# Two attentions in one queue: another order of their events, the selection's last steps among them, squares by ScalarE

## The chip, the cores and the metric

One core of one Trainium2 chip. The kernel is a single launch; its time is the device time in microseconds (us), the median of several runs. Before the change three runs took 2541.43, 2534.55 and 2539.69 us, median 2539.69 us.

## The reference

Two transformer blocks, one after the other, on 1024 tokens of width 1024, all in float32. The change lies in the first block, in two of its three mixers:

```
h = x @ w_in                                   # all mixers' inputs
# differential attention: 4 heads, 2 maps of 64 columns each, values 128 wide
p = softmax(q k^T * scale - slope * |i - j|, chunk-causal mask)      # per map
attn = p[map 0] - lam * p[map 1]
o = rms_norm(attn @ v over 128 columns, subln_g) * (1 - lam_init)
# sparse attention: 4 heads of 64 columns
score = sum over 8 heads of w_i * relu(q_i k_i^T)
sel = the 256 best keys of each query by score # blocks 0 and 1 take all their keys
out = softmax(q k^T * scale - slope * |i - j|, over sel) @ v
x = layer_norm(a * x + concat(gmlp, o, out) @ w_out)
```

Behind this stand a gated feed-forward layer and the whole second block; neither is touched.

## The kernel before

Each engine has its own program, written out by hand: `pe_program` (TensorE), `act_program` (ScalarE), `dve_program` (VectorE), `pool_program` (GpSimd) and `sp_program` (SyncE, which issues all DMAs). An engine works its program strictly in order; waits on semaphores tie them together. Queries are worked in 8 blocks of 128; block i sees 128 (i + 1) keys.

The stage before the attentions projects x (48 steps, `pe_project`) and beside that finds each query's 256th best score bit by bit (`dve_topk`). When the threshold of a query is known, `dve_choose` turns the scores of a block into a bias, block by block for i = 2 to 7: five VectorE instructions (lines 1194 to 1208) that mark ties, count them by a running sum, drop those that are too many, and write 0 or a large negative number plus the distance over the scores. Blocks 2 to 5 are done at the end of `dve_topk`, with `running` as their buffer; blocks 6 and 7 inside the attention loop, one instruction at each place from the second on, with `tcum` as buffer.

The attentions are 48 events: 32 differential ones ("b", head, block) and 16 sparse ones ("c", pair of heads, block). Every event has two maps: in "b" the two maps of a head, in "c" the two heads of a pair. The list `events` gives each event its place t. Each engine goes through places 0 to 54, and at place t it does different steps of several events:

- TensorE (`pe_attend`): the logits of event t, both maps (line 1296); the product with the values of event t - 4 (line 1386); the turning over (transposes) of event t - 2 (line 1360).
- VectorE (`dve_attend`): the logits' bias, scale and row maximum for each map of event t (line 1321), which empties TensorE's banks; the scaling of a sparse event t - 4 (line 1410), between the two maps; the reciprocal of the sums of event t - 1 and, for "b", the joining of its two maps (lines 1338 to 1346); for a head whose last block was 5 places ago the mean squares (lines 1419 to 1423, with `tcum`), and 6 places ago the scaling of its whole output (line 1440).
- ScalarE (`act_attend`): the exponentials of event t (line 1330), the scaling of a "b" event t - 4 (line 1400), the copies of the turned maps of event t - 2 (line 1372), and a square root 5 places behind a head's last block (line 1428).
- SyncE (`sp_attend`): first the loads of heads 1 and 4, then, 5 places behind, the stores of finished sparse outputs and further loads of heads, 6 places behind the stores of a finished head; behind the last head's stores the loads of the mixed blocks (`sp_mix_in`).

A "b" event turns one map (the joined one), a "c" event two. The banks are two rings: logits in 4 banks, turned maps and products in 4. An event of more than 512 keys takes all 4 banks of the first ring. The values of a map lie in one of eight buffers `vals`, which together are `res`.

The operands of a head (queries and keys in two parts each, and values) are five loads of 512 KB into one of three stacks (`sp_load_head`, lines 1277 and 1279): differential heads n = 0 to 3 into stacks 0 and 1 in turn, the two sparse pairs, n = 4 and 5, into stack 2. TensorE waits for all five before an event's logits (`pe_logits`, line 1287). Head 0 is loaded in the stage before. The loads of heads 1 and 4 stand behind the projection's last stores, first head 1, then head 4.

Behind the attentions `pe_mix` turns the mixed blocks that come back from DRAM: block 0 before the last event's product, the others behind it.

Of the kernel before, what the change touches and what calls it, by code (L numbers as in the profile page):

```python
# [166 lines left out]
def rest(*streams):  # L167
    for s in streams:
        for _ in s:
            pass  # L170


def build(nc, T, out):
    with ExitStack() as top:
# [91 lines left out]
        junk = sb("junk", 1024, BF, 512)  # L266
        junk_a = sb("junk_a", 1024, BF, 512)
        sg, powers = sb("sg", 128), sb("powers", 32)
        running = res[:, 7168:8192]


        area(low)
# [879 lines left out]
        def dve_topk():  # L1152


            dve.wait_ge(*BITS_BANK["r"].prior("bits"))
            for n, i in BY_DVE + BY_ACT:
                dve.i.memset(limit[:, n:n + 1], cols[i][1] - (256.0 if n < 3 else 512.0)).then_inc(*dv.up())
            dve.i.tensor_copy(bits, powers[:, 0:31].bitcast(U32)).then_inc(*dv.up())
            dve_count(BY_DVE + BY_ACT, None, ALU.is_ge)
            dve.wait_ge(*dv.now())  # L1160
            dve.i.tensor_scalar(ci, cnt, 256.0, -1.0, ALU.is_lt, ALU.mult).then_inc(*dv.up())
            dve.wait_ge(*dv.now())
            dve.i.tensor_tensor(cu, cu, bits[:, 30:31].broadcast_to([128, 6]), ALU.bitwise_xor).then_inc(*dv.up(("threshold", 30)))
            for b in BITS:
                dve_count(BY_DVE, cand[:, 0:6], ALU.is_lt)
                dve.wait_ge(*av.after(("signs", b)))
                dve.wait_ge(*dv.now())
                dve.i.tensor_tensor(rj, cnt, limit, ALU.is_gt).then_inc(*dv.up())
                dve.wait_ge(*dv.now())
                dve.i.scalar_tensor_tensor(out=cu, in0=rj, scalar=b, in1=cu, op0=ALU.logical_shift_left, op1=ALU.bitwise_xor  # L1170
                                           ).then_inc(*dv.frees(uses, "bits"))
                if b:
                    dve.wait_ge(*dv.now())
                    dve.i.tensor_tensor(cu, cu, bits[:, b - 1:b].broadcast_to([128, 6]), ALU.bitwise_xor
                                        ).then_inc(*dv.up(("threshold", b - 1)))
                yield
            dve_next_up()
            dve_count(BY_DVE + BY_ACT, cand[:, 0:6], ALU.is_gt)
            dve.wait_ge(*dv.now())
            dve.i.tensor_scalar(need, cnt, -1.0, 256.0, ALU.mult, ALU.add).then_inc(*dv.up())  # L1180
            yield
            for i in range(2, 6):
                rest(dve_choose(i, running))
                yield
            while True:
                yield

        def dve_choose(i, sums):

            n = COLUMN[i]  # L1190
            o, ln = cols[i]
            sc, thr, jk = score[:, o:o + ln], cand[:, n:n + 1], junk[:, 0:ln]
            dve.wait_ge(*dv.now())
            dve.i.tensor_scalar(jk, sc, thr, None, ALU.is_equal).then_inc(*dv.up())
            yield
            dve.wait_ge(*dv.now())
            dve.i.tensor_tensor_scan(sums[:, 0:ln], jk, jk, 0.0, ALU.add, ALU.bypass).then_inc(*dv.up())
            yield
            dve.wait_ge(*dv.now())
            dve.i.scalar_tensor_tensor(out=jk, in0=sums[:, 0:ln], scalar=need[:, n:n + 1], in1=jk, op0=ALU.is_gt,  # L1200
                                       op1=ALU.mult).then_inc(*dv.up())
            yield
            dve.wait_ge(*dv.now())
            dve.i.scalar_tensor_tensor(out=sc, in0=sc, scalar=thr, in1=jk, op0=ALU.is_lt, op1=ALU.add).then_inc(*dv.up())
            yield
            dve.wait_ge(*nd_in.after("nd"))
            dve.wait_ge(*dv.now())
            dve.i.scalar_tensor_tensor(out=sc, in0=sc, scalar=-BIG, in1=nd[:, 896 - 128 * i:1024], op0=ALU.mult, op1=ALU.min
                                       ).then_inc(*dv.up(("chosen", i)))
            yield  # L1210
# [3 lines left out]

        b_events = [("b", h, i) for h in range(4) for i in range(8)]
        c_events = [("c", p, i) for p in range(2) for i in range(8)]
        events = b_events[0:8]

        events += [e for pair in zip(b_events[8:16], c_events[0:8]) for e in pair] + b_events[16:20]
        events += [e for pair in zip(b_events[20:24], b_events[24:28]) for e in pair]  # L1220
        events += [e for pair in zip(b_events[28:32], c_events[8:12]) for e in pair] + c_events[12:16]
        N_EVENT = len(events)
        place_of = {e: t for t, e in enumerate(events)}
        turned_uses = [(t, m) for t, e in enumerate(events) for m in range(1 if e[0] == "b" else 2)]
# [167 lines left out]
        def act_outputs(t):  # L1392
            kind, g, i = events[t]
            tile = (t, "out")
            act.wait_ge(*dv.after((t, "rc")))
            act.wait_ge(*mm.after((t, 0, "out")))
            for k in range(4):
                act.wait_ge(*stage_out[k].after(("v", CV0 + 4 + k)))
            act.wait_ge(*osb_out[g % 2].after(("b", g - 2)))
            act.i.activation(osb[g % 2][:, 128 * i:128 * i + 128], uses.held[tile][:, 0:128], ACT.Copy,  # L1400
                             scale=small((t, "rc"), 2)[:, 0:1]).then_inc(*av.frees(uses, tile))

        def dve_outputs(t):
            kind, g, i = events[t]
# [7 lines left out]
                                rc.unsqueeze(2).broadcast_to([128, 2, 64]), ALU.mult).then_inc(*dv.frees(uses, tile))  # L1412


        def dve_subln(h):
            ss, ob = small(("subln", h), 24), osb[h % 2]
            dve.wait_ge(*av.after((place_of["b", h, 7], "out")))
            dve.wait_ge(*dv.now())
            dve.i.tensor_tensor(tcum[:, :], ob[:, :], ob[:, :], ALU.mult).then_inc(*dv.up())
            dve.wait_ge(*dv.now())  # L1420
            dve.i.tensor_reduce(ss[:, 0:8], tcum.rearrange("p (n c) -> p n c", n=8), AX.X, ALU.add).then_inc(*dv.up())
            dve.wait_ge(*dv.now())
            dve.i.tensor_scalar(ss[:, 0:8], ss[:, 0:8], 1.0 / 128, LN_EPS, ALU.mult, ALU.add).then_inc(*dv.up(("subln_var", h)))

        def act_subln(h):
# [61 lines left out]

        def dve_attend():

            last_choices = chain(dve_choose(6, tcum), dve_choose(7, tcum), repeat(None))  # L1490
            for t in range(N_PLACES):
                if t < N_EVENT:
                    dve_logits(t, 0)
                u = lagging(t, 4, "c")
                if u is not None:
                    dve_outputs(u)
                if t < N_EVENT:
                    dve_logits(t, 1)
                u = lagging(t, 1)
                if u is not None:  # L1500
                    dve_sums(u)
                    next(last_choices)
                h = last_block(t, 5)
                if h is not None:
                    dve_subln(h)
                h = last_block(t, 6)
                if h is not None:
                    dve_subln_end(h)
# [1428 lines left out]
```

## Time and profile before

| | |
|---|---|
| runs, median (lowest to highest) | 2539.69 us (2534.55 to 2541.43) |
| profiled execution, its own time | 2536.39 us |
| its span | 2534.4 us |
| TensorE, VectorE, ScalarE, GpSimd busy | 2403.1, 1491.6, 944.3, 688.5 us |
| TensorE's mean granted clock | 0.976 of full speed |
| attention stage, first logits to last product | 345 to 567 us |

The clock column of a window (PEclk) is the TensorE clock that was granted, as a share of the full 2.4 GHz; 0.50 is 1.2 GHz. Busy time of TensorE at half clock is twice that of the same work at full clock. A row of a timeline gives the start from the span's beginning, the length, the engine, line and operation, and in brackets how long the engine had been idle and what ended that.

### The profile page before, as it was taken

The page shows a single profiled execution, that of the slowest core. Times are in us where ns is not written, and L with a number is a line of the kernel's source. Part 1 is how long each engine was busy: PE and PEld are TensorE (multiplying, and loading weights), DVE is VectorE, ACT ScalarE, POOL GpSimd, SP SyncE. Part 2 cuts the span into 40 slices and gives each one's busy share as a digit, 9 for nine tenths or more (in the row PEclk, how much of TensorE's full clock was granted, in tenths as well). Part 3 has the DMA queues.
Part 4 walks back from the last instruction along what each step waited for, and adds up shares of the span by engine and source line. Part 5 has one row for each costly group of instructions (what it writes and reads, how often), then busy time and mean ns, then how long its engine had stood idle before and what let it go on. Part 6 is the DMA issues. An engine that isn't in the chain of part 4 may idle for free.

```text
span 2534.4 us, 31471 instructions
## 1 busy us (share of the span) xinstructions
PE 2403.1 (95%) x12119; PEld 1944.2 (77%) x12119; DVE 1491.6 (59%) x2500; ACT 944.3 (37%) x1762; POOL 688.5 (27%) x389
## 2 busy tenths in 40 slices
PE   8999968889999999999999989888989999999998
PEld 6678857777887777778887866666868888888887
DVE  3588998762766777753239037775476555544225
ACT  3467836661223232222113225553433233332112
POOL 3022210001135445542223211012224444442220
PEclk9999978999999999999999999998989999999999
DMA  5026441224215455454222210001332222233233
GB/s 173 9 64 195 161 156 56 96 66 147 103 56 154 154 158 158 146 202 166 91 100 75 75 42 18 26 18 67 100 94 73 84 75 92 84 133 117 100 108 116
DMA packets 216860, 260.00 MB, mean 103 GB/s; under 512 B 16364, under 2 KB 145916, under 8 KB 216712
## 3 DMA queue, kind: packets, MB, share of 16 engines
q1 hardware_dynamic: 216712, 258.00, 31.0%
q8 instruction: 96, 1.57, 0.3%
q14 instruction: 52, 0.43, 0.1%
HBM read 198.14 MB, written 59.82 MB: 102 GB/s over the span
## 4 chain that ended last, share of the span: by engine, by line
PE 55%; DVE 8%; DMA 2%; ACT 1%; issue 1%; POOL 1%; POOLq 0%; SPq 0%; DVEq 0%; ACTq 0%
PE bank L545 8%; PE bank L546 8%; PE bank L547 8%; PE bank L1878 7%; PE bank L1879 7%; PE bank L1880 7%; DVE rest L2498 3%; PE bank L521 2%; PE bank L523 2%; PE bank L522 2%; DMA early<-in_w_cond 1%; DVE took L2503 1%; DVE macc L1675 1%; POOL wl L502 1%; PE bank L2426 1%
## 5 line engine op out<-in xcount | busy, mean ns | idle before, releaser
L502 POOL TENSOR_TENSOR wl<-raw,wh 128x1024 fp32r<-128x1024 f32 x117 | 296.5, 2550 | 1338.8 <-ACT wh L485 1318.8
L545 PE MATMUL bank<-wh,yh 128*128 128x512 f32 x768 | 301.6, 393 | 3.7 <-POOL wl L502 1.7
L546 PE MATMUL bank<-wl,yh 128*128 128x512 f32 x768 | 299.5, 390 | 0.0
L547 PE MATMUL bank<-wh,yl 128*128 128x512 f32 x768 | 299.5, 390 | 0.0
L485 ACT ACTIVATE wh<-raw 128x1024 fp32r<-128x1024 f32 x117 | 123.2, 1057 | 311.0 <-PE bank L547 292.1
L497 POOL TENSOR_TENSOR wl<-res,wh 128x512 fp32r<-128x512 f32 x144 | 198.4, 1400 | 147.0 <-ACT wh L482 126.7
L1878 PE MATMUL bank<-yh,wh 128*128 128x512 f32 x576 | 225.2, 391 | 0.0
L1880 PE MATMUL bank<-yh,wl 128*128 128x512 f32 x576 | 224.1, 389 | 0.0
L1879 PE MATMUL bank<-yl,wh 128*128 128x512 f32 x576 | 224.1, 389 | 0.0
L497 POOL TENSOR_TENSOR wl<-raw,wh 128x512 fp32r<-128x512 f32 x108 | 156.3, 1461 | 232.1 <-ACT wh L482 232.1
L2077 DVE TENSOR_TENSOR res<-bank,res 128x512 f32<-128x512 f32 x96 | 65.6, 690 | 192.2 <-PE bank L547 192.2
L2011 DVE TENSOR_TENSOR res<-bank,res 128x512 f32<-128x512 f32 x144 | 99.6, 692 | 132.2 <-PE bank L1880 124.5
L545 PEld LDWEIGHTS bank<-wh,yh 128*128 128x128 f32 x768 | 144.6, 188 | 35.8 <-issue 5.4
L547 PEld LDWEIGHTS bank<-wh,yl 128*128 128x128 f32 x768 | 144.5, 188 | 30.2
L546 PEld LDWEIGHTS bank<-wl,yh 128*128 128x128 f32 x768 | 144.7, 188 | 29.2
L521 PE MATMUL bank<-yh,wh 128*128 128x512 f32 x384 | 153.6, 400 | 9.8 <-DVE yl L582 8.3
L482 ACT ACTIVATE wh<-res 128x512 fp32r<-128x512 f32 x144 | 83.4, 623 | 192.5 <-DVE res L469 141.4
L523 PE MATMUL bank<-yh,wl 128*128 128x512 f32 x384 | 150.8, 393 | 0.0
L522 PE MATMUL bank<-yl,wh 128*128 128x512 f32 x384 | 150.7, 392 | 0.0
L1878 PEld LDWEIGHTS bank<-yh,wh 128*128 128x128 f32 x576 | 108.1, 188 | 30.0 <-issue 4.3
L1880 PEld LDWEIGHTS bank<-yh,wl 128*128 128x128 f32 x576 | 108.1, 188 | 22.7
L1879 PEld LDWEIGHTS bank<-yl,wh 128*128 128x128 f32 x576 | 108.1, 188 | 22.1
(343 smaller groups left out, 5395.9 us busy)
## 6 DMA issues: line engine op xcount, KB each, us to landing
early<-in_w_cond SPq DMA_DIRECT2D x96, 256.0 KB, 3.0
raw<-in_w_gu SPq DMA_DIRECT2D x44, 512.0 KB, 4.2
raw<-in_w_down SPq DMA_DIRECT2D x44, 512.0 KB, 3.6
raw<-in_w_in SPq DMA_DIRECT2D x40, 512.0 KB, 4.1
qk_d<-res SPq DMA_DIRECT2D x36, 512.0 KB, 4.2
raw<-in_w_gate SPq DMA_DIRECT2D x22, 512.0 KB, 4.1
raw<-in_w_up SPq DMA_DIRECT2D x22, 512.0 KB, 4.3
res<-in_x SPq DMA_DIRECT2D x16, 512.0 KB, 10.0
```

Source lines behind the costliest of these rows:

```text
L485: act.i.activation(wh[n % NU][:, :], raw_of(u)[:, :], ACT.Copy).then_inc(*av.up(("wh", u)))
L497: pool.i.tensor_tensor(wl[n % NU][:, half], src, wh[n % NU][:, half].bitcast(F32), ALU.subtract).then_inc(*po.up(("wl", u)))
L502: pool.i.tensor_tensor(wl[n % NU][:, :], raw_of(u)[:, :], wh[n % NU][:, :].bitcast(F32), ALU.subtract).then_inc(*po.up(("wl", u)))
L521: pe.i.matmul(bank[:, :], a, a_h[:, s], start=k == 0, stop=False)
L522: pe.i.matmul(bank[:, :], a, a_l[:, s], start=False, stop=False)
L523: last = pe.i.matmul(bank[:, :], b, a_h[:, s], start=False, stop=k == 7)
L545: pe.i.matmul(bank[:, 0:wide], xa, h[:, c:c + wide], start=k == 0, stop=False)
L546: pe.i.matmul(bank[:, 0:wide], xa, l[:, c:c + wide], start=False, stop=False)
L547: last = pe.i.matmul(bank[:, 0:wide], xb_, h[:, c:c + wide], start=False, stop=k == nk - 1)
L1878: pe.i.matmul(bank[:, :], h[:, c:c + 128], high[:, k, :], start=k == 0, stop=False)
L1879: pe.i.matmul(bank[:, :], h[:, c:c + 128], low[:, k, :], start=False, stop=False)
L1880: last = pe.i.matmul(bank[:, :], l[:, c:c + 128], high[:, k, :], start=False, stop=k == 3)
```

## The change

The order of the events: two differential ones and one sparse one from the first place on, through places 0 to 23; then head 2's first six blocks alone; then again two to one, and the last three sparse events alone. The choices of blocks 2 to 5 leave `dve_topk` and join those of blocks 6 and 7 in the attention loop: 30 instructions, handed out at places 5 to 22 by `chosen_by`, all with `tcum` as buffer. VectorE takes the logits of both maps before it scales a sparse event's output. The squares of a differential head's output and their sums are no longer two VectorE instructions on the whole head, but one ScalarE activation with accumulation for each event, beside the one that scales it.

```diff
--- before.py
+++ after.py
@@ -266,7 +266,6 @@
         junk = sb("junk", 1024, BF, 512)
         junk_a = sb("junk_a", 1024, BF, 512)
         sg, powers = sb("sg", 128), sb("powers", 32)
-        running = res[:, 7168:8192]
 
 
         area(low)
@@ -1179,9 +1178,6 @@
             dve.wait_ge(*dv.now())
             dve.i.tensor_scalar(need, cnt, -1.0, 256.0, ALU.mult, ALU.add).then_inc(*dv.up())
             yield
-            for i in range(2, 6):
-                rest(dve_choose(i, running))
-                yield
             while True:
                 yield
 
@@ -1214,11 +1210,10 @@
 
         b_events = [("b", h, i) for h in range(4) for i in range(8)]
         c_events = [("c", p, i) for p in range(2) for i in range(8)]
-        events = b_events[0:8]
-
-        events += [e for pair in zip(b_events[8:16], c_events[0:8]) for e in pair] + b_events[16:20]
-        events += [e for pair in zip(b_events[20:24], b_events[24:28]) for e in pair]
-        events += [e for pair in zip(b_events[28:32], c_events[8:12]) for e in pair] + c_events[12:16]
+
+
+        events = [e for n in range(8) for e in (b_events[2 * n], b_events[2 * n + 1], c_events[n])] + b_events[16:22]
+        events += [e for n in range(5) for e in (b_events[22 + 2 * n], b_events[23 + 2 * n], c_events[8 + n])] + c_events[13:16]
         N_EVENT = len(events)
         place_of = {e: t for t, e in enumerate(events)}
         turned_uses = [(t, m) for t, e in enumerate(events) for m in range(1 if e[0] == "b" else 2)]
@@ -1397,8 +1392,11 @@
             for k in range(4):
                 act.wait_ge(*stage_out[k].after(("v", CV0 + 4 + k)))
             act.wait_ge(*osb_out[g % 2].after(("b", g - 2)))
-            act.i.activation(osb[g % 2][:, 128 * i:128 * i + 128], uses.held[tile][:, 0:128], ACT.Copy,
-                             scale=small((t, "rc"), 2)[:, 0:1]).then_inc(*av.frees(uses, tile))
+            bank, rc = uses.held[tile], small((t, "rc"), 2)[:, 0:1]
+            act.i.activation(osb[g % 2][:, 128 * i:128 * i + 128], bank[:, 0:128], ACT.Copy, scale=rc).then_inc(*av.up())
+            act.wait_ge(*av.now())
+            act.i.activation(junk_a[:, 0:128], bank[:, 0:128], ACT.Square, scale=rc,
+                             accum_out=small(("subln", g), 24)[:, i:i + 1]).then_inc(*av.frees(uses, tile))
 
         def dve_outputs(t):
             kind, g, i = events[t]
@@ -1412,14 +1410,10 @@
                                 rc.unsqueeze(2).broadcast_to([128, 2, 64]), ALU.mult).then_inc(*dv.frees(uses, tile))
 
 
+
         def dve_subln(h):
-            ss, ob = small(("subln", h), 24), osb[h % 2]
+            ss = small(("subln", h), 24)
             dve.wait_ge(*av.after((place_of["b", h, 7], "out")))
-            dve.wait_ge(*dv.now())
-            dve.i.tensor_tensor(tcum[:, :], ob[:, :], ob[:, :], ALU.mult).then_inc(*dv.up())
-            dve.wait_ge(*dv.now())
-            dve.i.tensor_reduce(ss[:, 0:8], tcum.rearrange("p (n c) -> p n c", n=8), AX.X, ALU.add).then_inc(*dv.up())
-            dve.wait_ge(*dv.now())
             dve.i.tensor_scalar(ss[:, 0:8], ss[:, 0:8], 1.0 / 128, LN_EPS, ALU.mult, ALU.add).then_inc(*dv.up(("subln_var", h)))
 
         def act_subln(h):
@@ -1487,19 +1481,23 @@
 
         def dve_attend():
 
-            last_choices = chain(dve_choose(6, tcum), dve_choose(7, tcum), repeat(None))
+            choices = chain.from_iterable(dve_choose(i, tcum) for i in range(2, 8))
+
+            def chosen_by(t):
+                return min(30, max(0, 5 * (t - 4) // 3))
+
             for t in range(N_PLACES):
                 if t < N_EVENT:
                     dve_logits(t, 0)
+                    dve_logits(t, 1)
                 u = lagging(t, 4, "c")
                 if u is not None:
                     dve_outputs(u)
-                if t < N_EVENT:
-                    dve_logits(t, 1)
                 u = lagging(t, 1)
                 if u is not None:
                     dve_sums(u)
-                    next(last_choices)
+                    for _ in range(chosen_by(t) - chosen_by(t - 1)):
+                        next(choices)
                 h = last_block(t, 5)
                 if h is not None:
                     dve_subln(h)
```

## Rows read from the trace of the kernel before

**Rows 1.** The page, part 1: busy time of each engine over the span

```profile
PE 2403.1 (95%) x12119; PEld 1944.2 (77%) x12119; DVE 1491.6 (59%) x2500; ACT 944.3 (37%) x1762; POOL 688.5 (27%) x389
```

**Rows 2.** Windows: length; busy PE, PEld, DVE, ACT, POOL; PEclk; DMA share; GB/s

```profile
345.40:362.20 16.80, 0.53 (x10) 0.33 (x6) 16.38 (x16) 2.33 (x4) 4.88 (x2) 0.61 0.69 249
362.20:402.00 39.80, 32.30 (x191) 25.62 (x192) 37.53 (x103) 23.33 (x67) 0.00 (x0) 0.69 0.16 57
402.00:453.00 51.00, 45.39 (x339) 37.22 (x338) 38.56 (x124) 36.70 (x86) 0.00 (x0) 0.90 0.22 71
453.00:503.00 50.00, 43.64 (x332) 36.07 (x332) 36.44 (x128) 34.28 (x90) 0.00 (x0) 0.93 0.35 119
503.00:547.00 44.00, 38.13 (x290) 31.57 (x290) 33.84 (x109) 33.24 (x78) 0.00 (x0) 0.92 0.06 19
547.00:567.00 20.00, 17.90 (x146) 17.76 (x147) 4.97 (x17) 7.99 (x16) 0.00 (x0) 0.91 0.42 142
```

**Rows 3.** Timeline of TensorE where the stage begins: start, length, idle before

```profile
362.48 0.69 PE L1296 MATMUL bank<-kh,qh 64*128 64x384 f32 x2 [16.55 <-DVE st L1321]
```

**Rows 4.** Timeline of the DMA issues of SyncE in the same stretch

```profile
354.60 3.44 SPq L1277 DMA_DIRECT2D qh<-qk_d  x1
...
359.52 0.43 SPq L1279 DMA_DIRECT2D v<-v_d  x1
```

**Rows 5.** Windows of 2 us, where the DMA engines fall quiet

```profile
368.00:370.00 2.00, 0.92 (x6) 0.23 (x6) 1.96 (x7) 0.90 (x3) 0.00 (x0) 0.50 0.18 47
```

**Rows 6.** Timeline of VectorE through the choices of blocks 2 to 5

```profile
340.01 0.42 DVE L1194 TENSOR_SCALAR junk<-score,cand 128x384 bf16<-128x384 f32 x1
...
345.22 2.86 DVE L1200 SCALAR_TENSOR_TENSOR junk<-res,cand,junk 128x512 bf16<-128x512 f32 x1
348.12 2.71 DVE L1204 SCALAR_TENSOR_TENSOR score<-score,cand,junk 128x512 f32<-128x512 f32 x1
...
360.96 0.96 DVE L1208 SCALAR_TENSOR_TENSOR score<-score,nd 128x768 f32<-128x768 f32 x1
```

**Rows 7.** Groups of VectorE's instructions from 340 to 567 us, shapes apart

```profile
L1419 DVE TENSOR_TENSOR tcum<-osb 128x1024 f32<-128x1024 f32 x4 | 4.9, 1225 | 0.4
L1421 DVE TENSOR_REDUCE st<-tcum 128x8 f32<-128x1024 f32 x4 | 4.9, 1220 | 0.1
...
L1410 DVE TENSOR_TENSOR osc<-bank,st 128x128 f32<-128x128 f32 x16 | 4.7, 291 | 27.5 <-PE bank L1386 27.5
```

**Rows 8.** Windows cut where TensorE's granted clock changes

```profile
379.00:389.00 10.00, 6.81 (x56) 5.43 (x52) 9.24 (x22) 6.11 (x13) 0.00 (x0) 0.96 0.01 2
389.00:396.00 7.00, 6.68 (x36) 5.97 (x36) 6.79 (x14) 4.25 (x12) 0.00 (x0) 0.57 0.00 0
...
420.00:470.00 50.00, 46.78 (x395) 40.92 (x396) 29.75 (x102) 32.58 (x79) 0.00 (x0) 0.99 0.12 40
```

**Rows 9.** Timeline of TensorE in the second half and at the end

```profile
475.52 0.47 PE L1296 MATMUL bank<-kh,qh 64*128 64x128 f32 x2 [4.05 <-DVE st L1321]
...
515.14 0.44 PE L1296 MATMUL bank<-kh,qh 64*128 64x384 f32 x2 [2.35 <-DVE st L1321]
...
551.22 2.79 PE L1386 MATMUL bank<-v,pt 128*128 128x64 f32 x24
...
560.53 1.94 PE L564 MATMUL bank<-con,ms 128*128 128x128 f32 x8 [1.70 <-DMA ms<-mix_d]
```

**Rows 10.** Timeline of VectorE: the last head's scaling

```profile
550.59 2.19 DVE L1440 SCALAR_TENSOR_TENSOR osb<-osb,st,sg 128x128 f32<-128x128 f32 x8
```

**Rows 11.** Groups of ScalarE's instructions from 345 to 567 us, shapes apart

```profile
L1330 ACT ACTIVATION_READ_ACCUMULATOR res<-res,st 128x1 f32 x96 | 18.2, 190 | 0.0
...
L1400 ACT ACTIVATE osb<-bank,st 128x128 f32<-128x128 f32 x32 | 11.3, 352 | 0.1
...
L1330 ACT ACT_TABLE_LOAD x4 | 5.1, 1283 | 0.1
```

**Rows 12.** Groups of ScalarE's instructions over the whole span

```profile
L631 ACT ACTIVATE sq<-res 128x1024 bf16<-128x1024 f32 x31 | 32.8, 1058 | 52.6 <-DVE res L2077 28.0 <-DVE res L2656 12.0 <-DVE res L627 11.9
```

## The prediction

> **What bounds the kernel now.** The page's first part [rows 1] shows TensorE busy for 2403.1 of 2534.4 us; the attention stage, the only place that the change touches, holds its longest pause. So I cut that stage into windows [rows 2], then read the timelines of TensorE [rows 3, 9], SyncE's issues [rows 4], the DMA engines [rows 5] and VectorE [rows 6, 7, 10] in it.
>
> Three stretches are to be seen. (a) 345.9 to 362.5: TensorE stands still for 16.55 us [rows 3], because VectorE makes the choices of blocks 2 to 5, from 340.01 to 361.92 [rows 6], before it touches the first logits. (b) Places 0 to 23 (heads 0 and 1 of the differential attention, head pair 0 of the sparse one), 362.2 to 453.0 us: VectorE is busy 37.53 + 38.56 = 76.1 of 90.8 us. TensorE is busy 32.30 + 45.39 us, but at mean clocks of 0.69 and 0.90; at full clock that is 32.30 x 0.69 + 45.39 x 0.90 = 63.1 us of work [rows 2]. VectorE binds here. (c) Places 24 to 47 and their tail, 453 to 567: VectorE 36.44 + 33.84 + 4.97 = 75.3 us, TensorE 40.6 + 35.1 + 16.3 = 92.0 us at full clock [rows 2], so TensorE binds, with gaps.
>
> **The change, part by part.** I take it as a shift of two times: when place 23 is done (453.0 before) and when the last sum over the values is done (567 before, the end of the last window; everything after hangs on it, and the code behind it is unchanged).
>
> *1. The first sparse event moves from place 9 to place 2.* Its operands are stack 2, head number 4. SyncE's program is unchanged: head 1's loads are issued first, head 4's behind them, from 354.60 to 359.95 [rows 4], and the DMA engines fall quiet within the window 368 to 370, whose mean share is only 0.18 [rows 5]: 0.4 us of full traffic in 2 us, so head 4 lands at about 368.4. Before, nobody waited for it, since all of head 0 stood ahead of the first sparse event. Now TensorE's queue holds at place 2, and behind it, in order, stand the turns and products of places 0 and 1 and all logits. The choices no longer hold TensorE, but the DMA does: it restarts at 368.4 instead of 362.5. Of the 16.55 us nothing is won; 368.4 - 362.2 = **+6.2 us** are lost in the start of stretch (b), and VectorE stands idle from about 347 to 368, since `chosen_by` hands it no choice before place 5. Only the logits of places 0 and 1 are done beforehand: two maps of 128 and two of 256 columns, at 0.29 us for 128 [rows 7] about 1.1 us of VectorE.
>
> *2. The choices of blocks 2 to 5 move into places 5 to 16.* From 340.01 to 361.92 they took 21.9 us. Two of them lasted 2.86 and 2.71 us [rows 6] while GpSimd worked beside them (4.88 us of it in that window [rows 2]); one of like form on 768 elements took 0.96 [rows 6], by length 0.64 and a fixed part, so on 512 I take 0.75: 5.57 - 1.50 = 4.1 us go, and 17.8 us of VectorE work stay and now lie in (b), where VectorE binds. Cover for them: the waits that VectorE has there. (b) has 90.8 - 76.1 = 14.7 us in which it isn't busy; part of this are the gaps between dependent instructions, which stay. I let 6.0 us be filled (bounds 0 and 10). The choices therefore cost **+11.8 us** (+7.8 to +17.8).
>
> *3. Squares by ScalarE.* Each head loses a product and a reduction on VectorE, 1.225 + 1.220 = 2.45 us [rows 7]. Head 0's falls in (b): with the 1.1 us of places 0 and 1, **-3.5 us**. Heads 1 and 2 in (c): TensorE's waits of 4.05 and 2.35 us [rows 9] stand right behind these two pairs, so I count both, **-4.9 us** (0 to -6.4). Head 3's is off the path. What is added: 32 activations of 128 columns, 0.35 us as the scaling beside them, and an accumulator read of 0.19 [rows 11]: 0.5 us each, 17 us in all on ScalarE, which is busy 23.33 + 36.70 + 34.28 + 33.24 = 127.6 of 185 us in (b) and (c) [rows 2]. It has room on the mean, but in its queue the copies of the turned maps stand behind each square, and the bank of the output is freed 0.5 us later. With about a third of 12 such events per half on the path: **+2 us** in (c), and under VectorE's cover in (b) (bounds 0 and +8 for both, were half of all on the path).
>
> *4. Both maps' logits before the sparse outputs.* VectorE waited 27.5 us for the products before these 16 multiplications [rows 7], with the second map's logits queued behind. In the window from 547 to 567, where no logits are left, it was busy 4.97 of 20 us [rows 2]; I put that idle time, 15 us, down to the last four of the 16. Of the 12.5 us left, about 4 in (b) are already in the 6.0 us of step 2. In (c) the wait itself remains, since VectorE still waits for the product; what is late next is `dve_sums`, which comes behind it. I take **-3 us** (0 to -8).
>
> *5. TensorE's clock in (b).* With steps 1 to 4, (b) ends at 368.4 + (90.8 + 11.8 - 3.5) = 467.5 us if VectorE alone binds: 99 us, in which TensorE has 62 us of full-clock work, 63% busy. At half clock the same work is 124 us, more than VectorE's. The rows show what follows: after 379 to 389 with TensorE busy 6.81 of 10 us the clock fell to half (0.57 in 389 to 396); from 420 to 470 it was busy 46.78 of 50 and kept 0.99 [rows 8]. Bounds: 0, and 124 - 99 = +25. In (b) before, 35 of 90.8 us ran at half clock (from 0.69 and 0.90) and VectorE still bound most of them. I expect half the stretch at half clock and take **+9 us**. The Trainium skill, "TensorE: Matmul & The Clock Gate", section "HAM oscillation", says that waits which come back in each turn of a loop throw the array back to half rate each time, and so speaks against a loop in which VectorE binds; by it, taken to the letter, the upper bound would be the price.
>
> *6. The tail.* Head 3's last block is at place 43 instead of 42, so its scaling comes behind one more wait for a sparse product. Before, the eight multiplications began at 550.59 [rows 10] and the first block came back from DRAM at 560.53, with 1.70 us of waiting [rows 9]: 9.9 us. Now they start behind the product that began at 551.22 and took 2.79, at about 554.3, so the block is there at 564.3: **+3.5 us** (0 to +5; head 3's squares, 2.45 us earlier, can give some of it back).
>
> Sum: place 23 ends at 467.5 + 9 = 476.5, +23.5 us. Stretch (c): -4.9 + 2 - 3 + 3.5 = -2.4. Together **+21 us**. On the profiled execution's own 2536.4 us (its span 2534.4 and 2.0 around it): 2557.4. It lies 3.3 us under the median of the shown runs, 2539.7; from that it would be 2560.7. I say **2558**.
>
> **The rivals.** *A. Same or nearly: the clock holds.* If TensorE keeps its full clock through (b) and the reordering gives all it can (-8 instead of -3), it is 21 - 9 - 5 = +7: 2543. For it: the waits become many short ones. Against it: rows 8.
>
> *B. Faster: one mix of kinds evens out stretch (c).* Before, heads 2 and 3 ran as pairs of differential events (places 28 to 35), then alternating, then four sparse ones alone. If two to one keeps both engines loaded, (c) tends to TensorE's 92.0 us instead of 114: up to -22 in place of -2.4. With (b) at its best, +14.5 without the clock term and 4.0 less where the choices fill 10 us of waits, that is 2536.4 + 10.5 - 22 = 2525; it decides as soon as (c) gains more than the 10.5 to 23.5 that (b) loses. For it: the gaps of 4.05 and 2.35 us. Against it: the last four places keep three sparse events in a row, places 24 to 29 are differential alone, and the tail is longer.
>
> *C. The clock stays low,* so that TensorE binds all of (b), as after each pause in rows 8: 21 - 9 + 25 = +37, 2574.
>
> *D. ScalarE reloads its table for each square.* In line 631's group 31 squares run beside roots with no load in their line [rows 12]; beside exponentials no row shows any. A switch to a root and back takes two loads of 1.283 us [rows 11]. 64 of them would be 82 us more on ScalarE: 127.6 + 17 + 82 = 227 us of work where the forecast has 368.4 to 568, 200 us: 27 us more at least, 40 with some of its waits kept, 2598. The Trainium skill, "ScalarE: Activation LUTs", section "Table sets: the hidden batching unit", has functions in named sets, cheap ones in every set, and would have each switch cost 2.66 us; by that figure 64 switches would be 170 us. It does not list squares among those in every set.
>
> *E. The change is void at the start:* stack 2 is there by place 2 and the 16.55 us go. Then VectorE's 99 us run from 346: 445 + 9 = 454, (c) -2.4: 2535. The issue times forbid it unless the loads are reordered, which the change doesn't do.
>
> **How the numbers follow.** Chances: forecast 0.62, A 0.12, B 0.08, C 0.11, D 0.03, E 0.04. What a measurement can tell from no change is 0.3%, 7.6 us. Range: low end between forecast and A, 2542; high end at C, 2574. Faster by over 0.3%: three quarters of B, 0.06. Within: A, E and the rest of B, 0.18. Slower: the forecast, C and D, 0.76.
>
> **What would show it.** Step 1: TensorE's first logits of place 2 wait about 22 us for a DMA, ending near 368; were the wait for VectorE or absent, step 1 is wrong and E right. Step 2: place 23's choices and logits on VectorE end between 467 and 485. Step 5: PEclk under 0.8 between 369 and 475; at 0.95 A holds. Steps 3 and 4: the stretch from place 24 to the last product lasts 109 to 114 us; under 100 is B. Step 6: the wait for the first mixed block exceeds 4 us. D: table loads at the line of the squares. The prediction is wrong if the last product ends before 574 us.

## The result, and the profile after

The changed kernel took 2558.58 us (median of 4 runs, 2553.1 to 2558.87), the kernel before 2537.89 us on the same chip (2534.55 to 2541.43): ratio 1.0082, 95% interval 1.0066 to 1.0099, 20.7 us slower. Here and below, a number for one kernel leaves out the rare execution that was far slower than its others (one of kernel d1, 3998.52 us, and one of the kernel before beside it, 4834.88 us). The span grew from 2534.4 to 2556.5 us; the engines' busy times hardly moved:

```profile
PE 2406.5 (94%) x12119; PEld 1949.4 (76%) x12119; DVE 1478.7 (58%) x2492; ACT 959.4 (38%) x1826; POOL 688.9 (27%) x389
```

VectorE has 12.9 us less and ScalarE 15.1 us more than in [rows 1]. So the time is waiting, and the windows of the attention stage tell where. They are cut at the restart of TensorE, at place 24 (VectorE's first logits of head 2), where VectorE begins the last map's logits, and at the end of the last product; columns as in [rows 2].

```profile
344.00:369.20 25.20, 0.84 (x14) 0.63 (x14) 2.74 (x11) 4.44 (x11) 4.66 (x2) 0.57 0.72 256
369.20:469.80 100.60, 79.58 (x534) 64.92 (x534) 89.17 (x235) 65.09 (x171) 0.00 (x0) 0.82 0.11 36
469.80:558.80 89.00, 77.52 (x599) 65.54 (x598) 62.68 (x225) 72.38 (x195) 0.00 (x0) 0.92 0.23 76
558.80:587.50 28.70, 22.77 (x165) 22.15 (x165) 5.01 (x22) 11.32 (x23) 0.00 (x0) 0.80 0.29 99
```

Before, the same three stretches lasted 90.8 (362.2 to 453.0), 91.1 (453.0 to 544.1) and 22.7 us (544.1 to 566.8) [rows 2 cuts them a little otherwise]. Place 24 is 16.8 us later; the second stretch is 2.1 us shorter, 89.0; the tail is 6.0 us longer, 28.7. Another 1.5 us lie between the last product and the first matrix product with `w_out` (10.4 before, 12.0 now). Together that is 22.2 us, and the span grew by 22.1: nothing changed behind.

The start, in TensorE's timeline, with the two longest of a new kind of wait (against [rows 3]):

```profile
369.18 0.47 PE L1291 MATMUL bank<-kh,qh 64*128 64x128 f32 x2 [24.36 <-DMA v<-v_d]
...
424.08 0.47 PE L1355 MATMUL bank<-con,res 128*128 128x128 f32 x1 [4.69 <-ACT junk_a L1398]
...
462.19 0.90 PE L1355 MATMUL bank<-con,res 128*128 128x128 f32 x3 [5.49 <-ACT junk_a L1398]
```

SyncE's issues of head 4 (against [rows 4]), and VectorE's timeline (against [rows 6]):

```profile
353.04 4.38 SPq L1272 DMA_DIRECT2D qh<-qk_d  x1
...
358.89 0.43 SPq L1274 DMA_DIRECT2D v<-v_d  x1
```

```profile
344.55 0.29 DVE L1316 CUSTOM_DVE_ANT_0 res<-bank,nd 128x128 f32<-128x128 f32 x1 [5.71 <-PE bank L1291]
...
347.72 1.02 DVE L1338 SCALAR_TENSOR_TENSOR st<-st,cand 128x1 f32<-128x1 f32 x1
348.78 0.35 DVE L1341 SCALAR_TENSOR_TENSOR res<-res,st 128x128 f32<-128x128 f32 x1
370.12 0.29 DVE L1316 CUSTOM_DVE_ANT_0 res<-bank,nd 128x128 f32<-128x128 f32 x1 [20.99 <-PE bank L1291]
```

```profile
469.83 0.28 DVE L1316 CUSTOM_DVE_ANT_0 res<-bank,nd 128x128 f32<-128x128 f32 x1
```

VectorE finishes place 0 at 349.1 and then stands for 20.99 us, since no choice is handed to it. The wait view of TensorE and VectorE from 345 to 590 (who waited <- for whom: us, times, longest; against [rows 7]):

```profile
DVE osc L1408 <- PE bank L1381: 30.3, 7, 12.8
...
PE bank L1291 <- DMA v<-v_d: 24.4, 1, 24.4
PE bank L1355 <- ACT junk_a L1398: 21.8, 9, 5.5
...
PE bank L563 <- DMA ms<-mix_d: 4.4, 1, 4.4
```

The row of line 1355 is new in size: 21.8 us, where TensorE before waited 3.2 us for the same banks:

```profile
PE bank L1360 <- ACT osb L1400: 3.2, 5, 0.8
```

ScalarE's timeline ahead of the wait that ended at 462.19 shows what it is made of:

```profile
458.63 1.15 ACT L1325 ACTIVATE res<-res,st 128x1024 f32<-128x1024 f32 x1 [3.54 <-DVE st L1316]
...
460.15 1.15 ACT L1325 ACTIVATE res<-res,st 128x1024 f32<-128x1024 f32 x1 [0.27 <-DVE st L1316]
...
461.29 0.35 ACT L1396 ACTIVATE osb<-bank,st 128x128 f32<-128x128 f32 x1
461.67 0.37 ACT L1398 ACTIVATE junk_a<-bank,st 128x128 bf16<-128x128 f32 x1
```

A sparse event of more than 512 keys takes four banks for its turning; the fourth of them still holds the output of a differential event (TensorE had done 11 of the 14 transposes, three banks full, and the last 3 waited until 462.19). ScalarE frees that bank only behind both exponentials of the running place. These wait for VectorE's logits, and those for VectorE's choices. The square itself is 0.4 us of it. In the old alternating order the output that stands in the ring at a sparse event's turning is a sparse one too, which VectorE frees; with two differential events to each sparse one it is ScalarE's. The end of the stage (against [rows 9]):

```profile
571.15 3.24 PE L1381 MATMUL bank<-v,pt 128*128 128x64 f32 x28
578.81 1.97 PE L563 MATMUL bank<-con,ms 128*128 128x128 f32 x8 [4.42 <-DMA ms<-mix_d]
580.57 6.93 PE L1381 MATMUL bank<-v,pt 128*128 128x64 f32 x32
...
599.45 0.48 PE L544 MATMUL bank<-wh,yh 128*128 128x512 f32 x1
```

TensorE waits 4.42 us for the first mixed block, and the last product then takes 6.93 us, at a granted clock of 0.50, 1.2 GHz (before: 1.70 us, 4.53 us and 0.81). The squares cost 0.56 us each, the read of the accumulator among it, and no table load: there are as many loads as before (against [rows 11, 12]):

```profile
L1398 ACT ACTIVATE junk_a<-bank,st 128x128 bf16<-128x128 f32 x32 | 11.8, 368 | 1.0
...
L1398 ACT ACTIVATION_READ_ACCUMULATOR junk_a<-bank,st 128x1 f32 x32 | 6.2, 193 | 0.0
...
L1325 ACT ACT_TABLE_LOAD x4 | 5.1, 1283 | 0.1
```

### The profile page after: what moved, and what is told of

It reads as the page before. It is cut to its first block, busy times and chain, and to the rows that moved or that the text cites. A ratio compares the mean times of both kernels' runs of the same rounds, so it can differ in the third digit from the quotient of the medians.

```text
span 2556.5 us, 31537 instructions
## 1 busy us (share of the span) xinstructions
PE 2406.5 (94%) x12119; PEld 1949.4 (76%) x12119; DVE 1478.7 (58%) x2492; ACT 959.4 (38%) x1826; POOL 688.9 (27%) x389
## 4 chain that ended last, share of the span: by engine, by line
PE 78%; DVE 12%; DMA 3%; ACT 3%; issue 2%; POOL 1%; SPq 1%; POOLq 0%; DVEq 0%; ACTq 0%
PE bank L544 10%; PE bank L546 10%; PE bank L545 10%; PE bank L1876 7%; PE bank L1878 7%; PE bank L1877 7%; PE bank L520 5%; PE bank L522 5%; PE bank L521 5%; DVE rest L2496 2%; PE bank L1381 2%; DVE res L1316 2%; PE bank L1291 1%; PE bank L563 1%; DVE took L2501 1%
```

## The experiments

Kernels a and t are the changed kernel with one edit, d1 with four, kernels b the one before with one part of the change; c2, d2 and e1 keep the old order of events. Ratios are against the kernel before, measured beside each on the same chip, with 95% intervals; "place 24" and "last product" are read from the profiles (before: 453.0 and 566.8; changed: 469.8 and 587.5). From the first matrix product with `w_out` to the end, where no edit touches the code, the 14 profiled executions differ by up to 8 us (1955.4 to 1963.1), so a place in the stage tells an edit's worth better than the total of one execution.

**a1: head 4 loaded first.**

```diff
-            for n in (1, 4):
+            for n in (4, 1):
                 sp_load_head(n)
```

> The changed kernel with one edit: SyncE loads head 4 (the first sparse pair) before head 1. Theory of the prediction (TensorE's restart is set by head 4's arrival, and VectorE then binds to place 24, so a shift of the start is carried to the end): the first logits of place 2 move from 369.2 to about 362, the total falls by 7 us against the changed kernel, to about 2551. Rival 1 (the stretch is bound by the waits for banks behind ScalarE's queue, which absorb an earlier start): restart at 362, but total down by at most 3 us. Rival 2 (the restart wasn't held by this load): restart stays at 369.

1.0058 (1.0039 to 1.0076), 2552.2 us. TensorE's first row of place 2, and VectorE's first logits of place 24:

```profile
363.24 0.48 PE L1291 MATMUL bank<-kh,qh 64*128 64x128 f32 x2 [18.28 <-DMA v<-v_d]
```

```profile
462.96 0.28 DVE L1316 CUSTOM_DVE_ANT_0 res<-bank,nd 128x128 f32<-128x128 f32 x1
```

Restart 5.9 us, place 24 6.9 us, last product 6.7 us and the total 6.4 us earlier: the start is carried to the end in full. Rivals 1 and 2 fall.

**a2: choices into the wait.**

```diff
             def chosen_by(t):
-                return min(30, max(0, 5 * (t - 4) // 3))
+                return 0 if t < 1 else 20 + min(10, max(0, 2 * (t - 4) // 3))
```

> The changed kernel with one edit: 20 of the 30 steps of the choices (blocks 2 to 5) are handed out at place 1, where VectorE otherwise waits for head 4, the other ten over places 5 to 19. Theory of the prediction (17.8 us of choices lie in a stretch that VectorE binds): place 24 comes 10 to 14 us earlier, total 2545 to 2549. Rival (the waits for banks behind ScalarE's exponentials bind as much as VectorE): place 24 comes at most 6 us earlier, total 2552 or more.

1.0035 (1.0023 to 1.0047), 2546.2 us. VectorE's first logits of place 24:

```profile
456.01 0.28 DVE L1316 CUSTOM_DVE_ANT_0 res<-bank,nd 128x128 f32<-128x128 f32 x1
```

13.8 us earlier at place 24, 12.4 us in the total, although TensorE restarted at the same time (368.9). VectorE was busy 72.24 us from the restart to place 24, 16.9 us less than in the changed kernel, and 13.8 us of them came through: the choices cost most of what VectorE spends on them, as the theory had it.

**a3: the output's bank earlier.**

```diff
                     act_exp(t, 0)
-                    act_exp(t, 1)
                 u = lagging(t, 4, "b")
                 if u is not None:
                     act_outputs(u)
+                if t < N_EVENT:
+                    act_exp(t, 1)
```

> The changed kernel with one edit: ScalarE does the scaling and squares of event t-4 between the two exponentials of event t, not behind both, so the bank of the output is free earlier by one exponential. If the 21.8 us that TensorE waited for the bank behind the squares (9 times, up to 5.5 us) set the end, they fall by a third or more and the total by 5 to 9 us, to about 2551. If VectorE binds the first half anyway, only waits in the second half count: 1 to 3 us, total about 2556; worse than the changed kernel if the second exponential, now later, is what the turning waits for.

1.0063 (1.0042 to 1.0084), 2555.1 us. TensorE's wait in the wait view:

```profile
PE bank L1355 <- ACT junk_a L1398: 9.0, 5, 4.0
```

The wait fell from 21.8 to 9.0 us, place 24 moved by 0.6 us, the last product by 2.5 us and the total by 3.5 us. In the first half VectorE binds, and the 21.8 us were mostly a shadow of its lateness.

**b6: the new order alone.**

```diff
-        events = b_events[0:8]
-        events += [e for pair in zip(b_events[8:16], c_events[0:8]) ...
...
+        events = [e for n in range(8) for e in (b_events[2 * n], b_events[2 * n + 1], c_events[n])] + b_events[16:22]
+        events += [e for n in range(5) for e in ...
```

> The kernel before with one part of the change: the new order of events. The choices of blocks 2 to 5 stay ahead of the loop, blocks 6 and 7 one step at each place, squares on VectorE, sparse outputs between the two maps. Theory of the prediction: VectorE makes the choices while TensorE would wait for head 4 anyway, so of the loss only the start (6 to 7 us) and the tail (3 to 4 us) remain: 2537.9 + 10 = 2548. Rival (the order itself is bad, because a sparse event's turning waits for a bank held by a differential one): 2555 or more. Rival (the order evens out the second half, as rival B of the prediction has it): 2536 or less.

1.0052 (1.0031 to 1.0073), 2552.3 us. The wait view of TensorE:

```profile
PE bank L1293 <- DMA v<-v_d: 24.0, 1, 24.0
...
PE bank L1357 <- ACT osb L1397: 11.4, 7, 4.5
```

Place 24 at 462.7, 9.7 us later than before, where 6 to 7 were expected; last product at 582.8, 16 us later. The waits for banks grow without a square too (11.4 us; before 3.2): the order alone lengthens them. The total of about 2548 was too low by 4 us; neither rival is reached, and the median lies between the 2548 of the theory and the 2555 of the first rival.

**b7: squares by ScalarE alone** (the change's lines in `act_outputs` and `dve_subln`).

> The kernel before with one part of the change: squares by ScalarE. VectorE loses 2.45 us four times, twice with TensorE waiting right behind it. Prediction's step 3: -4.9 us and -2.45 in the first half, +2 for the later banks: total 2532 to 2534. Rival (ScalarE's 17 us cost as much as VectorE's 10 give): 2536 to 2539.

0.9992 (0.9978 to 1.0006), 2535.6 us: the rival's side, no difference that can be measured. Place 24 came at 450.6, 2.5 us earlier, head 0's two instructions exactly; the last product at 564.7, so of heads 1 and 2 nothing came through. TensorE's wait for the banks in the wait view:

```profile
PE bank L1360 <- ACT junk_a L1403: 10.3, 9, 3.0
```

So the squares lengthen it too, without the order: 10.3 us for 3.2. What became of heads 1 and 2 can be read in TensorE's timeline, first of b7, then (last line) of the kernel before at the same step:

```profile
511.02 0.44 PE L1296 MATMUL bank<-kh,qh 64*128 64x384 f32 x2
...
515.35 1.13 PE L1360 MATMUL bank<-con,res 128*128 128x128 f32 x4 [2.96 <-ACT junk_a L1403]
```

```profile
517.24 1.17 PE L1360 MATMUL bank<-con,res 128*128 128x128 f32 x4 [0.59 <-ACT osb L1400]
```

The logits behind head 2's squares came at 511.02 instead of 515.14, 4.1 us earlier, without the wait of 2.35 us. The turning behind them then waited 2.96 us for a bank, and 1.9 us were left: ScalarE had loaded a table, taken head 2's root and loaded the table back (509.57 to 512.38) before the exponentials, the scaling and the square that free that bank.

**b8: sparse outputs behind both maps' logits, alone** (the change's lines in `dve_attend`).

> The kernel before with one part of the change: sparse outputs are scaled behind both maps' logits. Prediction's step 4: 3 us to be won in the second half and some in the first, where events alternate: 2531 to 2534. Rival (VectorE waits for the same product, only later, and the sums behind it are late): no change, 2535 to 2538.

0.9975 (0.9962 to 0.9987), 2530.1 us, better than expected. VectorE's first logits of place 24:

```profile
447.60 0.29 DVE L1321 CUSTOM_DVE_ANT_0 res<-bank,nd 128x128 f32<-128x128 f32 x1
```

5.4 us earlier there, 5.7 at the last product: the gain lies in the first half. The profiled execution (2536.42 us) was the slowest of the twelve and lost these 5.7 us again behind the stage; the ratio rests on all twelve.

**b9: choices inside the loop, alone, in the old order.**

```diff
-            for i in range(2, 6):
-                rest(dve_choose(i, running))
-                yield
...
+            choices = chain.from_iterable(dve_choose(i, tcum) for i in range(2, 8))
+
+            def chosen_by(t):
+                return min(30, max(0, 5 * (t - 3) // 2 - 15 if t > 12 else t - 2))
...
+                    for _ in range(chosen_by(t) - chosen_by(t - 1)):
+                        next(choices)
```

> The kernel before with one part of the change: the choices of blocks 2 to 5 inside the loop, spread over places 3 to 17, in the old order of events. Prediction's step 2 without the load's wait: VectorE's chain doesn't get shorter by the 17.8 us, it only loses the 4.1 us beside GpSimd and fills some of its waits: 4 to 8 us won, 2528 to 2532. From the runs so far (all parts in the old order -8.8, squares -0.1, sparse outputs behind -5.6) the difference would be -3: 2532 to 2534. Rival (the 16.55 us of TensorE's wait go as a whole): 2520 to 2524.

1.0002 (0.999 to 1.0013): nothing won, less than the 4 to 8 us that were expected, and nothing of the rival's 16.55 us. The window from TensorE's second start, at place 0's turning, to place 24:

```profile
350.20:456.20 106.00, 85.61 (x522) 70.00 (x522) 91.35 (x238) 58.99 (x145) 0.00 (x0) 0.76 0.26 91
```

TensorE's logits of place 2 start at 346.31 instead of 362.48, place 0's turning at 350.32 instead of 363.94, and place 24 is 3.2 us later. VectorE is busy 91.35 of 106 us, so it stands for 14.7 us, as long as before (362.2 to 453.0): no wait was filled. TensorE gets a mean clock of 0.76 (before 0.81).

**c2: the whole change, but the old order** (with b9's `chosen_by`).

> The changed kernel with the order of events taken back to that of before (head 0 alone first, then alternating, pairs of differential events, four sparse ones last); everything else of the change stays, the 30 steps of the choices spread over places 3 to 21. Theory: what the change loses comes from the order (it wants head 4 at place 2, and it lengthens the tail), while the moved choices free the start: TensorE isn't held at 346, VectorE's chain starts at 344.5 instead of 340 plus 21.9, place 24 comes 5 to 10 us earlier than before, the tail is as before, total 2526 to 2532. Rival (VectorE's work is the same wherever the choices stand, and the waits for banks behind ScalarE's squares grow): within 3 us of before, 2534 to 2540.

0.9971 (0.9956 to 0.9987), 2526.9 us. The same window (its turning of place 0 starts at 349.73):

```profile
349.60:446.50 96.90, 78.40 (x523) 63.82 (x523) 88.83 (x236) 65.12 (x174) 0.00 (x0) 0.82 0.29 100
```

Place 24 at 446.5, last product at 555.4. VectorE is busy nearly as long as in b9, but waits 8.1 instead of 14.7 us. The single parts b7, b8 and b9 add up to 0.9969, so within their intervals they are independent in the old order. The new order, with the hand-out of choices that goes with it, turns this gain of 7 us into a loss of 21. By itself (b6) it costs 13 us; the other 15 us come from order and moved choices together: in b6 VectorE makes the choices of blocks 2 to 5 while TensorE waits for head 4, in the changed kernel that wait is empty, and a2, which fills it again, takes 12.4 us back.

**t1: head 3 finished one place earlier.**

```diff
+        events[41:44] = [events[42], events[43], events[41]]
         N_EVENT = len(events)
```

> The changed kernel with one sparse event (pair 1, block 3) moved behind head 3's last two blocks, which so finish at place 42, as before the change. Theory of the tail: from the last logits to the last product it took 28.7 us, before 22.7, because head 3's outputs are stored one place later, the first mixed block is waited for (4.4 us), and the last product then runs at half clock. With the edit the wait falls under 2 us, the last product runs at full clock and the total falls by 4 to 6 us, to about 2553. Rival (the tail is long for another reason, the stores of SyncE or the sparse products): less than 2 us.

1.0066 (1.0051 to 1.0081), 2553.6 us. TensorE at the end:

```profile
574.63 1.09 PE L563 MATMUL bank<-con,ms 128*128 128x128 f32 x8 [0.41 <-DMA ms<-mix_d]
575.56 3.68 PE L1382 MATMUL bank<-v,pt 128*128 128x64 f32 x32
```

The wait is 0.41 us, the last product takes 3.68 us, and from the last logits to the last product it is 21.5 us instead of 28.7. The granted clock is 1.00 in both rows. The total fell by 5.0 us by the medians, 4 by the ratios.

**d1: the new order with all repairs** (a1, a3, t1, and 15 steps of the choices at place 1).

> The changed kernel in its new order with all four repairs at once: head 4 loaded before head 1, 15 steps of the choices (blocks 2 to 4) at place 1, ScalarE's scaling between the exponentials, head 3 finished one place earlier. If the terms found one by one add up (-6.4, -12.4 less about 4 for block 5 that no longer fits into the shorter wait, -3.5, -5), the total is 2558.6 - 23 = about 2536, as before the change: the order itself then gives nothing. Rival A (two to one evens out the engines once the start is mended): 2530 or less. Rival B (the repairs overlap, since each takes the same idle time): 2541 or more.

0.9947 (0.9933 to 0.9962), 2528.2 us: rival A, not the sum. From just behind the restart (364.2) to place 24:

```profile
365.20:452.00 86.80, 72.72 (x539) 58.85 (x539) 77.53 (x221) 64.60 (x174) 0.00 (x0) 0.91 0.18 61
```

With the first microsecond that is 87.7 us instead of 100.6; the clock is 0.91 instead of 0.82. The last product ends at 558.1, 29.4 us earlier than in the changed kernel, of which 17.8 us lie ahead of place 24 and 11.6 behind. The medians are 30.4 us apart and the ratios 34 (the kernel before ran at 2540.2 beside d1, 2.3 us above what the changed kernel was measured against); the span of d1's profile, 2531.4 us, is only 25.1 us shorter, since 6 us were lost behind the stage. So the repairs together give 6 to 11 us more than the 23 us of their sum. By which step they help each other is open.

**d2: c2 with a3's edit.**

> The kernel with the old order and all else of the change (2526.9 us), with one more edit: ScalarE scales and squares between the two exponentials. On the changed kernel that edit gave 3.5 us. Theory: TensorE still waits 10.2 us in 9 pieces for banks behind the squares; a third to half of it goes and is carried to the end: total 2522 to 2525. Rival (VectorE binds, and the later second exponential costs what the earlier bank gives): 2526 to 2529.

0.9942 (0.9929 to 0.9956), 2526.8 us. Its median is c2's and so on the rival's side; its ratio is lower by 0.0029, against a kernel before that ran slower beside it, and its last product is 1.2 us earlier, its place 24 1.0 us later (447.5): what the edit gives here is not settled between 0 and 7 us.

**e1: d2 with the choices of blocks 2 to 5 ahead of the loop again.**

> The kernel with the old order, squares by ScalarE between the two exponentials and sparse outputs behind both maps, but with the choices of blocks 2 to 5 ahead of the loop, as before the change. Against its twin with the choices inside the loop (0.9942 of before) it tells what moving them is worth. Theory: VectorE binds the first half, so moving its work within it gives only the 4.1 us beside GpSimd and some filled waits, and the choices alone gave nothing (1.0002): this kernel stands within 5 us of its twin, 0.994 to 0.996 of before. Rival (TensorE's wait of 16.55 us at the start is worth most of its length once the rest is mended): 0.998 or more.

0.9952 (0.9936 to 0.9968), 2524.2 us. From the end of the projection to the end of these choices TensorE stands still as before:

```profile
345.00:362.00 17.00, 0.42 (x8) 0.24 (x6) 16.58 (x18) 2.51 (x4) 4.75 (x2) 0.63 0.75 264
```

Place 24 at 447.2, last product at 552.9, against 447.5 and 554.2 in d2. So moving the choices was worth nothing that can be measured, twice (b9, e1), and the best versions are d2, e1 and d1, 12 to 15 us under the kernel before and not told apart.

## Why the prediction was right

Direction, size and the main cause held: +21 us were forecast, +20.7 measured. But that the sum is so near is luck: its first half was forecast 6.7 us too high, its second half and tail 6.3 us too low. Two of the prediction's own signs failed with these terms: the clock was to be under 0.8 up to 475 (0.82 to place 24), and place 24 to the last product was to last 109 to 114 us (117.7).

- *Step 1, head 4 at place 2, +6.2 us:* shown. The wait ended at 369.18 for 368.4, the DMA is named in the row, and a1 moved restart and total together.
- *Step 2, the choices, +11.8 us:* shown. VectorE was busy 89.17 us from the restart to place 24, where the working had 76.1 + 17.8 - 3.5 = 90.4; a2 took 20 of the 30 steps out and place 24 came 13.8 us earlier.
- *Step 3, squares:* head 0's 2.45 us came in full in b7; the -4.9 and +2 in the second half were 0 together (from place 24 to the last product 114.1 us in b7, 113.8 before). b7's lead over the kernel before went from 2.5 us at place 24 only to 4.1 behind head 2's squares, and the wait of 2.96 us for a bank that ScalarE freed late brought it back to 1.9. The waits for banks, +2 us in the working, grew by 7.1 us in b7 (10.3 for 3.2), so that term was sized too low; how much of the 7.1 lay on the path is open. ScalarE's price per square was as reckoned (0.56 us for 0.5).
- *Step 4:* -3 us forecast in the second half, -5.7 measured, nearly all in the first, where I had counted it as cover for the choices.
- *Step 5, the clock, +9 us:* the step that failed in size. VectorE alone would have reached place 24 at 467.5 by the prediction's sum; it was 469.8, of which 0.8 us is the later restart, so clock and banks together are left with 1.5 us. This is an estimate, since it leans on the 6.0 us of cover of step 2. VectorE's own waits bound it without that (its wait view from 369.2 to 469.8):

```profile
DVE res L1316 <- PE bank L1291: 23.4, 5, 21.0
DVE osc L1408 <- PE bank L1381: 2.1, 1, 2.1
```

Of these, 21.0 us are the wait that ended at 370.12. The rest, 2.4 + 2.1 = 4.5 us, is all that VectorE lost to a late TensorE on the way to place 24, for whatever reason; before it was 5.0 + 4.9 = 9.9 us (362.2 to 453.0). TensorE did get only 0.82 and waited for banks, but both lay nearly whole beside VectorE's work. It went to and fro between its two levels of clock, 1.2 and 2.4 GHz, as its windows of 5 us show (columns as above; the clock is the last but two):

```profile
420.00:425.00 5.00, 0.92 (x3) 0.68 (x5) 4.79 (x14) 4.70 (x12) 0.00 (x0) 0.76 0.62 202
425.00:430.00 5.00, 4.57 (x24) 3.56 (x22) 4.64 (x19) 1.84 (x5) 0.00 (x0) 0.50 0.35 107
430.00:435.00 5.00, 5.00 (x28) 4.82 (x25) 3.23 (x10) 3.48 (x10) 0.00 (x0) 0.50 0.01 3
435.00:440.00 5.00, 5.00 (x27) 4.15 (x27) 4.15 (x6) 0.60 (x1) 0.00 (x0) 0.53 0.04 13
440.00:445.00 5.00, 2.51 (x23) 2.00 (x23) 4.68 (x11) 4.19 (x11) 0.00 (x0) 1.00 0.00 0
...
460.00:465.00 5.00, 2.81 (x13) 2.09 (x15) 4.26 (x8) 3.69 (x9) 0.00 (x0) 0.52 0.00 0
```

The clock fell while TensorE waited the 4.69 us that ended at 424.08, and again in the wait of 5.49 us that ended at 462.19. Behind the first it stayed at half clock up to 439, though TensorE was busy almost without a pause. The Trainium skill, "TensorE: Matmul & The Clock Gate", section "HAM oscillation", describes a fall to half rate behind waits that come back, and these rows agree with the fall; but the price that it would have here, the prediction's upper bound, didn't come, since the slow matmuls lay beside VectorE's work.

- *Step 6, the tail, +3.5 us:* +6.0 measured. The delay itself came as reckoned: the wait for the first mixed block ended 18.3 us later than before (578.81 for 560.53), 3.6 us more than the 14.7 us by which the tail began later. Missed was the clock: during the wait of 4.42 us it fell to 0.50 and stayed there, so the last product takes 6.93 us, 2.4 us more than before.
- *Place 24 to the last logits* (the terms of steps 3 and 4 in the second half): -5.9 forecast, -2.1 measured.

The second half and the tail cost 6.3 us more than forecast (3.8 and 2.5), the first half 6.7 us less (16.8 for 23.5, nearly all of it the clock's), and 1.5 us came behind the last product. By luck the total is therefore better than its parts.

Of the rivals, A was nearly right on what the clock costs in (b), though not on why (the clock did not hold, 0.82), and the gains it took from the reordering weren't there. B did not come about in the change (its case against itself was even understated: the new order keeps four sparse events in a row at its end, as the old one does, not three); in d1, with start and tail mended, the new order reached 0.9947, no better than the old one with a3's edit (d2, 0.9942). C, D and E are excluded by the rows.

## What to carry to other kernels

When work is reordered, look up for each step that comes earlier when its operands land, not only when they were waited for: a load that no one ever waited for (here head 4's, at 368 us) can be the next thing to bind. A long idle stretch of the busiest engine can be worth nothing (b9 and e1: no difference that can be measured) if the work that filled it on the other engine is only moved further down that engine's own critical queue. And put a step that is moved into a known wait of its engine, as a2 does, not at a schedule counted from its consumers.

## What the runs showed of the hardware that had not been expected

- The last product, the same 32 records, took one of two lengths in 13 of the 14 profiles. Behind a wait for the mixed block of at most 1.45 us (b7, b9, c2, d1, d2, e1, t1) it took 3.68 us at a granted clock of 1.00; behind 1.86 us (b8) and behind 4.32 to 4.56 us (the changed kernel, a1, a2, a3, b6) it took 6.93 us at 0.50. Only the kernel before, with 1.70 us, lies between (4.53 us, 0.81). So a wait ahead of this burst cost up to 3.25 us more than its own length, and behind 4.32 to 4.56 us of waiting no more than behind 1.86 us.
- A VectorE instruction on a single column, 0.22 us at 370.74, took 1.02 us at 347.72, up to 348.74, while GpSimd worked on its 1024 columns up to 348.73; in [rows 6] two of 512 elements took 2.86 and 2.71 us in that place.
